# Hybrid attention and mLSTM layer in fp32: order of the first head's weights, issuer of the caches, one bias request for each mLSTM head, GpSimd parts of two chunks

## The reference

```python
h = rmsnorm(x, g_pre); p = h @ w_in + b_in
q_a,k_a,v_a,z_a, q_m,k_m,v_m,o_m,z_m, i_m,f_m, g_a,g_b = split(p)
att = sliding_window_attention(rope(q_a), rope(k_a), v_a, sinks, meta keys, window 128)   # 16 heads, 4 kv heads
hm  = mlstm(q_m, k_m, v_m, i_m, f_m)          # 4 heads of 256, matrix state, chunks of 128
y_a = att * silu(z_a); y_m = sigmoid(o_m) * hm * silu(z_m)
merged = sigmoid(g_a) * (y_a @ w_pa) + sigmoid(g_b) * (y_m @ w_pb)
x = x + rmsnorm(merged @ w_out, g_post)
```

## Time and profile before

| | |
|---|---|
| median of 3 runs | 3042.82 us (3042.74 to 3046.93) |
| the profiled execution, its own time | 3043.17 us |
| its span | 3041.4 us |
| PE busy | 2953.9 us (97%) |
| DVE, ACT, POOL busy | 1462.1, 1065.7, 1295.3 us |
| attention, mLSTM, tail begin at about | 0, 947, 2167 us of the span |

### The profile page before, as it was taken

One profiled execution on the slowest core, in us unless ns is written; L12 is line 12 of the kernel. 1 busy time (PEld: TensorE's weight loads), 2 busy tenths in 40 slices (PEclk: granted clock), 3 DMA queues, 4 the chain that ended last, 5 costly groups with the idle time before them and its releaser, 6 DMA issues. The chain is left out here.

```text
span 3041.4 us, 48151 instructions
## 1 busy us (share of the span) xinstructions
PE 2953.9 (97%) x16722; PEld 2546.8 (84%) x16722; DVE 1462.1 (48%) x3600; ACT 1065.7 (35%) x2460; POOL 1295.3 (43%) x939
## 2 busy tenths in 40 slices
PE   6999999999999999999999999999899999999998
PEld 5998998998996888788878887888688887878787
DVE  4665554555453332533353335332354655556587
ACT  4775544544543211321132113111233223333343
POOL 2223321321322454545444545451354434456576
PEclk9999999999999999999999999999899999999999
DMA  7222212112313744474446534632446666396843
GB/s 210 93 83 83 66 54 78 60 53 82 88 53 109 230 160 146 144 220 165 135 154 203 182 125 155 229 132 87 158 166 239 240 226 230 123 332 216 311 160 131
DMA packets 261043, 464.67 MB, mean 153 GB/s; under 512 B 29715, under 2 KB 143016, under 8 KB 256949
## 3 DMA queue, kind: packets, MB, share of 16 engines
q1 hardware_dynamic: 240276, 399.34, 39.3%
q10 hardware_dynamic: 17824, 53.06, 4.8%
q0 software_dynamic: 2720, 9.32, 1.0%
HBM read 307.25 MB, written 156.38 MB: 152 GB/s over the span
## 5 line engine op out<-in xcount | busy, mean ns | idle before, releaser
L277 POOL TENSOR_TENSOR a_all<-h_raw,a_all 128x1024 fp32r<-128x1024 f32 x137 | 337.8, 2466 | 743.1 <-issue 454.5
L286 PE MATMUL bank_first<-w_all,a_all 128*128 128x384 f32 (+1 forms) x1088 | 417.2, 383 | 7.5 <-DVE ml_qk L632 4.7
L288 PE MATMUL bank_first<-w_all,a_all 128*128 128x384 f32 (+1 forms) x1088 | 395.4, 363 | 0.0
L287 PE MATMUL bank_first<-w_all,a_all 128*128 128x384 f32 (+1 forms) x1088 | 394.9, 363 | 0.0
L535 ACT ACTIVATE ml_qkt<-ml_pt 128x512 f32<-128x512 f32 x68 | 40.7, 598 | 922.3 <-PE ml_pt L805 922.3
L2554 DVE TENSOR_TENSOR a_all<-tl_sums,a_all 128x512 fp32r<-128x512 f32 x165 | 181.3, 1101 | 171.0 <-ACT a_all L2426 169.9
L286 PEld LDWEIGHTS bank_first<-w_all,a_all 128*128 128x128 f32 x1088 | 204.8, 188 | 62.2 <-issue 38.5
L632 DVE TENSOR_TENSOR ml_qk<-bank_first,ml_bias 128x512 f32<-128x512 f32 x68 | 47.0, 692 | 381.1 <-ACT ml_kw L539 373.6
L286 PE MATMUL bank_second<-w_all,a_all 128*128 128x512 f32 x544 | 220.1, 405 | 3.3 <-issue 3.3
L288 PEld LDWEIGHTS bank_first<-w_all,a_all 128*128 128x128 f32 x1088 | 204.6, 188 | 22.1
L287 PEld LDWEIGHTS bank_first<-w_all,a_all 128*128 128x128 f32 x1088 | 205.0, 188 | 19.5
(11 more groups left out here) (445 smaller groups left out, 7967.4 us busy)
## 6 DMA issues: line engine op xcount, KB each, us to landing
w_split<-w_early SPq DMA_DIRECT2D x140, 512.0 KB, 3.3
h_raw<-h_t SPq DMA_DIRECT2D x121, 512.0 KB, 4.4
w_all<-w_split SPq DMA_DIRECT2D x34, 1024.0 KB, 14.2
stage<-w_in_in SPq DMA_DIRECT2D x42, 512.0 KB, 6.2
w_rest<-w_split SPq DMA_DIRECT2D x16, 1024.0 KB, 9.7
w_early<-w_split SPq DMA_DIRECT2D x14, 1024.0 KB, 8.2
h_t<-h_raw SPq DMA_DIRECT2D x17, 512.0 KB, 5.7
y_t<-at_yt SPq DMA_DIRECT2D x68, 128.0 KB, 2.2
```

What stands on the lines that cost most here:

```text
L277: nc.gpsimd.tensor_tensor(k.h_lo[:, u], k.h_raw[:, u], k.h_hi[:, u].bitcast(F32), ALU.subtract).then_inc(k.h_lo_ready, 1)
L286: nc.tensor.matmul(out, hi[:, j], k.w_hi[:, j, col:col + n], start=(j == 0), stop=False)
L287: nc.tensor.matmul(out, hi[:, j], k.w_lo[:, j, col:col + n], start=False, stop=False)
L288: last = nc.tensor.matmul(out, lo[:, j], k.w_hi[:, j, col:col + n], start=False, stop=(j == KT - 1))
```

## The change

- The chunks of attention group 0 come in the order z, z, q's second half, k with v, q's first half; PE's first block_b waits for 2 chunks. ACT's and DVE's lists at the start are put in that order, with the gates' columns ahead of chunk 1.
- SP asks for rcos, rsin and the sinks ahead of the fifth chunk and of x 3. It no longer asks for the caches, smask and perm: POOL does, between its low parts of h tiles 0 and 1, in 8 requests (kwin and vwin in two halves each).
- `load_bias` of the mLSTM part is one request for all five rows.
- At a change of mLSTM head POOL makes the low parts of chunks 6 and 7 (after chunks 0 to 3 are made), DVE those of 4 and 5; ACT makes the high part of the h tile ahead of chunks 2 and 3; `prepared` gives POOL's tile 15 of heads 0 to 2 no share, and all later shares move back a step for each. SP's wait for the stored weights moves from tile 12 to tile 14 of the last head.

```diff
 STG = 4
+POOL_CHUNKS = (6, 7)
...
     b = attn_base(n)
-    return [("w_in", q + P, b + P), ("kv", n, b + 2 * P), ("w_in", z, b + 3 * P), ("w_in", z + P, b + 4 * P),
-            ("w_in", q, b)]
+    qk, zs = [("w_in", q + P, b + P), ("kv", n, b + 2 * P)], [("w_in", z, b + 3 * P), ("w_in", z + P, b + 4 * P)]
+    return (qk + zs if n else zs + qk) + [("w_in", q, b)]
...
+def lower_count(k, c):
+
+    i = c - k.ML[1]
+    if i >= 0 and 4 <= i % 10 <= POOL_CHUNKS[-1]:
+        return c - i % 10 + POOL_CHUNKS[-1] + 1
+    return c + 1
+
+
 def load_chunk(eng, k, c):
...
         eng.wait_ge(k.w_hi_ready, former[-1] + 1)
-        eng.wait_ge(k.w_lo_ready, former[-1] + 1)
+        eng.wait_ge(k.w_lo_ready, lower_count(k, former[-1]))
     slot = staged(k, c)
...
-            unit, part = (n - 1) // 3, (n - 1) % 3
-            if n < 1 or unit >= N_PASS * KH:
+            resting = [NT * h + NPT - 1 for h in range(MH - 1)]
+            step = n - 1 - sum(r < n for r in resting)
+            unit, part = step // 3, step % 3
+            if n < 1 or n in resting or unit >= N_PASS * KH:
                 return ()
...
-            for i, c in enumerate((C_QM, C_KM, C_VM, C_OM, C_ZM)):
-                eng.dma_start(bias[:, h % 2, i * MD:(i + 1) * MD],
-                              k.b_in[0:1, c + h * MD:c + (h + 1) * MD].to_broadcast([P, MD])).then_inc(bias_in[h % 2], 16)
+            src = k.b_in[0:1, C_QM:C_QM + 5 * D].rearrange("o (i n) -> o i n", n=D)[:, :, h * MD:(h + 1) * MD]
+            eng.dma_start(bias[:, h % 2].rearrange("p (i n) -> p i n", n=MD),
+                          src.to_broadcast([P, 5, MD])).then_inc(bias_in[h % 2], 16)
...
                         load_block(sp, k, 0, T2, part, early_in)
-                if t == 12:
+                if t == 14:
                     for s in prep_out:
...
                 nc.scalar.activation(wexp[:, :], wlog[:, :], ACT.Exp).then_inc(wexp_ready, 1)
-                splits(h, t, "c")
                 if not (is_last(t) and h == MH - 1):
                     act_split_h(nc, k, u, 16 * (half + 27 + u), (proj_c, n + 1))
+                splits(h, t, "c")
                 splits(h, t, "end")
...
                     pool_split_h(nc, k, BASE + n + 2, u, (proj_c, n + 1))
+                if t == NPT - 1 and h + 1 < MH:
+                    pool.wait_ge(k.w_lo_ready, k.ML[h + 1] + 4)
+                    for c in POOL_CHUNKS:
+                        split_lo(pool, k, k.ML[h + 1] + c, k.chunks[k.ML[h + 1] + c][2])
                 for c in prepared(n):
...
             def evict_a(h, n):
-                dve.wait_ge(bias_in[h % 2], 80 * (h // 2 + 1))
+                dve.wait_ge(bias_in[h % 2], 16 * (h // 2 + 1))
                 dve.wait_ge(proj_a, n + 1)
...
                 for block_free, count, c in split_plan(h, t, part):
+                    if c - k.ML[h + 1] in POOL_CHUNKS:
+                        continue
+                    if c - k.ML[h + 1] == POOL_CHUNKS[-1] + 1:
+                        dve.wait_ge(k.w_lo_ready, c)
                     dve.wait_ge(block_free, count)
...
             load_x(2)
-            load_chunk(sp, k, STG)
-            load_x(3)
             sp.dma_start(rcos[:, :, :], k.c_rcos).then_inc(c_in, 16)
...
                          allow_slow_non_contiguous=True).then_inc(c_in, 16)
+            load_chunk(sp, k, STG)
+            load_x(3)
             sp.dma_start(headrow, k.c_headrow).then_inc(c_in, 16)
...
             store_h(0)
-            for i, (dst, src) in enumerate(((kwin, k.cache_win_k), (vwin, k.cache_win_v))):
-                sp.dma_start(dst[:, :, :], src[0].rearrange("b w h d -> w b (h d)")).then_inc(cache_in, 16)
-                if i == 0:
-                    store_h(1)
-            for dst, src in ((kmeta, k.cache_meta_k), (vmeta, k.cache_meta_v)):
-                sp.dma_start(dst[:, :], src[0].rearrange("b w h d -> (b w) (h d)")).then_inc(cache_in, 16)
-            sp.dma_start(smask[:, :, :], k.c_smask).then_inc(cache_in, 16)
-            sp.dma_start(perm[:, :, :, :], k.c_perm).then_inc(cache_in, 16)
+            store_h(1)
...
             pool_split_h(nc, k, 0, 0, None)
+            for dst, src in ((kwin, k.cache_win_k), (vwin, k.cache_win_v)):
+                for b in (0, NB // 2):
+                    half = slice(b, b + NB // 2)
+                    pool.dma_start(dst[:, half, :], src[0, half].rearrange("b w h d -> w b (h d)")).then_inc(cache_in, 16)
+            for dst, src in ((kmeta, k.cache_meta_k), (vmeta, k.cache_meta_v)):
+                pool.dma_start(dst[:, :], src[0].rearrange("b w h d -> (b w) (h d)")).then_inc(cache_in, 16)
+            pool.dma_start(smask[:, :, :], k.c_smask).then_inc(cache_in, 16)
+            pool.dma_start(perm[:, :, :, :], k.c_perm).then_inc(cache_in, 16)
             pool_split_h(nc, k, 1, 1, None)
...
             evict_h(0)
+            act.wait_ge(gate_in[0], 16)
+            nc.scalar.activation(k.w_hi[:, :, gate_cols], S["wif"][:], ACT.Copy).then_inc(gate_hi, 1)
+            split_made(0, None)
             act_split_chunk(nc, k, 1)
-            split_made(0, None)
+            evict_h(1)
             for c in range(2, 4):
                 act_split_chunk(nc, k, c)
-            act.wait_ge(gate_in[0], 16)
-            nc.scalar.activation(k.w_hi[:, :, gate_cols], S["wif"][:], ACT.Copy).then_inc(gate_hi, 1)
-            evict_h(1)
+            split_made(1, None)
             act_split_chunk(nc, k, 4)
             square(2)
-            split_made(1, None)
             evict_h(2)
...
             scale(1)
+            evict_h(0)
             dve_split_chunk(nc, k, 0)
-            evict_h(0)
-            for c in range(1, 4):
-                dve_split_chunk(nc, k, c)
             dve.wait_ge(gate_hi, 1)
...
                             ALU.subtract).then_inc(gate_lo, 1)
+            dve_split_chunk(nc, k, 1)
             evict_h(1)
-            dve_split_chunk(nc, k, 4)
+            for c in range(2, 5):
+                dve_split_chunk(nc, k, c)
             scale(2)
...
                 n0, d0 = PE_N * a, DVE_N * a
-                dve.wait_ge(cache_in, 16 * 6)
+                dve.wait_ge(cache_in, 16 * 8)
                 for i in range(2):
...
                 if new:
-                    pe.wait_ge(k.w_hi_ready, k.AT[a] + 4)
-                    pe.wait_ge(k.w_lo_ready, k.AT[a] + 4)
+                    pe.wait_ge(k.w_hi_ready, k.AT[a] + (4 if a else 2))
+                    pe.wait_ge(k.w_lo_ready, k.AT[a] + (4 if a else 2))
                 ready(a, m, u, z_ready)
...
                 kc = slice(HD * a, HD * (a + 1))
-                pe.wait_ge(cache_in, 16 * 6)
+                pe.wait_ge(cache_in, 16 * 8)
                 for b in range(NB):
```

## The result

The changed kernel takes 3055.42 us (median of 9 runs, 3046.45 to 3064.78), the kernel before 3042.82 (9 runs, 3037.09 to 3049.83): ratio 1.0039, 95% interval 1.0026 to 1.0051. It is slower by about 12 us, more than the 0.2% that can be told here, and outside the forecast range. The profiled execution took 3055.42 us, its span 3053.6.

What follows compares the result with a forecast made beforehand. PE was taken to bound the kernel, busy 2953.9 of 3041.4 us. Head changes -5.7, bias request -3.2 and start +1.2 made -7.7 us, giving 3035.0 us against the median of 3042.82; range 3029.5 to 3042.0.

Steps and rivals of the forecast that it cites:

- C, the caches: Start: POOL's four halves and perm each wait 4.0 us, caches there at 41.7; +1.2 us.
- rival 3: Start: GpSimd's requests each wait 8.1 us, or DVE blocks their writing; +21.7 us there, 3056 in all; chance 0.07.
- A start of L1879 after 45: Caches' transposes at the start: beginning before 39 or after 45 would show the reasons wrong; 41 to 43 expected.
- C: The start, first projection and caches' transposes together: +1.2 us, bounds -5.0 and +21.7.
- A: Three changes of mLSTM head: PE's two waits at each shrink, 1.9 us per change; -5.7 us.
- B: Start of the mLSTM part: one bias request lands sooner and the clock may stay up; -3.2 us.
- The estimate of 25 us for eight requests: Start: by the skill's figure for GpSimd DMA beside DVE, eight requests take 25 us; time near 3045.
- The same bytes have to be moved, whoever asks: Caches' loading at the start: DMA engines are full until about 40 in any order, the queue adding a little.
- C, the first projection: Start: block_b begins 2.9 us earlier, about 21.8, but block_a waits for the fifth chunk until 29.5; -0.5 left.
- Rival 4: Start of the mLSTM part: the single bias request moves no faster than five; -0.5 there, 3038 in all; chance 0.15.
- the first wait: Change of mLSTM head: PE's 0.93 us idle ahead of block_a, for POOL's h part; 0.85 counted as saved.
- the second: Change of mLSTM head: PE's 1.11 us wait ahead of block_b, for DVE's four chunks; 1.05 counted as saved.

Runs made afterwards that it cites:

- e3: The changed kernel with dynamic_dma_scratch_size 1280 in place of 1024, more room for GpSimd's descriptors; 3047.60 us against 3041.24 for the kernel before.
- e1: The changed kernel with SP again asking for the caches, smask and perm, as before; 3041.76 us against 3041.24 for the kernel before.
- e8: The changed kernel with GpSimd waiting, in the first attention head, for VectorE's at_qr before its chunk parts; 3053.20 us against 3043.11 for the kernel before.
- e6: The kernel before with only the start's new order (chunks, later fifth-chunk request, ACT's and DVE's lists); 3043.14 us against 3043.11.
- e12: e11 with the start's new order added; 3032.18 us against 3043.93 for the kernel before.
- e10: The kernel before plus the head-change part, GpSimd's wait for at_qr in all attention heads, and q/k bias rows on their own semaphore; 3033.05 us against 3043.28.
- e4: The kernel before with only the part at the changes of mLSTM head; 3038.82 us against 3041.24.
- e11: e10 with kwin and kmeta requested first, on their own semaphore; 3027.00 us (5 of 6 runs) against 3043.28 for the kernel before.

## Why the prediction was wrong

**C, the caches.** This step failed, and it decides. That "each of POOL's four halves and perm waits for the one before at 4.0 us" was the mechanism of rival 3 (0.07) with a time too small: 5 x 4.0 = 20 us, where the runs have 7.9, 5.4 and 4.4 us from half to half, 9.8 from the last half to perm's request, and 5.6 from there to PE, 33.2 in all. That made 54.87 of 41.7. The 9.8 us hold what the sum put at nothing: the three smaller requests, of which smask's landing held perm back. The 4.0 was taken from GpSimd's requests in the tail, 6 us or more apart; the 8.1 us landing in this stretch was the nearer row. A start of L1879 after 45 was the prediction's own sign of wrong reasons, and it came.

Rival 3's condition, x over 5.5 us, was met with (54.87 - 21.69) / 5 = 6.6. That its total of 3056 is close to the measured 3055.42 is luck: C cost 14.4 us and not 21.7, and A and B gave less than the 8.9 us it counted. The rival's second reason, that DVE keeps GpSimd from writing, is not borne out: the requests beside DVE's chunk parts took GpSimd 0.81 and 0.77 us, one with DVE idle 0.75, and e3 moved the standing by room alone. The estimate of 25 us for eight requests, from the Trainium skill ("SBUF — State Buffer", A bandwidth-pool intuition that's wrong), came near the 28.1 us that they took (21.69 to 49.81), also by luck: 5.3 us were issuing, 22.9 standing. "The same bytes have to be moved, whoever asks" was a wrong comfort: the queue on GpSimd, not the bytes, decided, as e1 shows. GpSimd's part of h tile 1 came at 49.83, not before 40.5, and cost nothing only because PE stood until 54.87 anyway.

**C, the first projection.** Block_b came at 22.92, not 21.8: DVE's part of chunk 1 took 2.56 us beside GpSimd's h part, where 1.23 was counted. Block_a came at 30.74, not 29.5. What was left out is the gap between them: in the change, e1, e3 and e8 the clock fell behind it and took more than the early start gave. In e6 and e12 it did not fall there, and the order still gave nothing in the end.

**B.** Not -3.2 but +0.8 in the trace. Rival 4 (0.15) had the kind: one request moves no faster, but it is worse than the -0.5 counted there. The one needs 8.1 us in the median to land, each of five 5.0. The clock stayed low too, since PE's wait did not shrink; in e10, where it did, the clock stayed up, as this step had supposed.

**A.** Right in kind and mis-sized: -5.7 predicted, -2.1 by the two traces and -2.4 in e4. Of the first wait, 0.3 us was saved and not 0.85: "1.8 us beside POOL" for DVE's part left out that one operation of DVE stands through GpSimd's whole h part (2.46 us). Of the second, 0.6 and not 1.05: DVE's two parts took 2.4 us each, not 1.8. The moved preparing and SP's later wait cost nothing that shows (e4's waits of L2710), as said.

**What was missing altogether.** The second hold near 267 us, 3.7 us in the changed kernel's profile. It had a row in before, a 2.33 us operation, and was not read, since the change does not touch it. A shift of the start was taken to carry everything behind it unchanged; in the traces it did not, where two engines start within 0.2 us of each other. In the medians this loss is not shown: e1 and e6 have it in their traces and equal the kernel before.

## What to carry to other kernels

Before requests are moved to GpSimd, look how many descriptors they have against the room set aside for it: several large ones in a row made it stand here, and a semaphore that counts them all together makes the consumer wait for the last. It was cheaper to wait only for what is used first (e11) than to move who asks. An operation of VectorE that takes ten times its usual length beside one of GpSimd is a hold; if TensorE waits for it, let GpSimd wait first. An earlier start that opens a gap behind it can give its gain back in clock, as in four of the six traces with this order.

## What the hardware showed unexpectedly

GpSimd's requests stand for 3.7 to 9.3 us (the change, e3) for want of descriptor room, each until an earlier one has landed, and 256 bytes more of it were worth 7 us. A fused bias request of 640 pieces lands after 8.1 us (7.1 to 11.0 over the traces), each of five of 128 pieces after 5.0. Where GpSimd's operations follow each other, VectorE can be held once or twice by them from the same 0.17 us distance; against none (12.8 us), one hold made the stretch 1.8 to 4.4 us longer and two made it 5.3 to 5.6, by how the clock went behind it.
